# The end of a mixture-of-experts stage: stored expert rows fetched and summed during the last expert, its own rows placed by one-hot products

## The reference

```python
def moe_swiglu(h, w_router, wg, wu, wd):
    logits = (h @ w_router).astype(jnp.float32)
    top_v, top_i = lax.top_k(logits, TOP_K)              # TOP_K = 2 of 8 experts
    w_top = jax.nn.softmax(top_v, axis=-1)
    gate = jnp.sum(jax.nn.one_hot(top_i, N_EXPERTS, dtype=jnp.float32) * w_top[..., None], axis=-2)
    out = jnp.zeros_like(h)
    for e in range(N_EXPERTS):
        out = out + gate[..., e:e + 1].astype(h.dtype) * swiglu(h, wg[e], wu[e], wd[e])
    return out

# in second_block, l = 1:
        h = layer_norm(ALPHA * h + f, ln2_g[l], ln2_b[l])   # f = moe_swiglu(h, ...)
```

## Time and profile before

| | us |
|---|---|
| median of 3 runs (lowest, highest) | 2637.42 (2636.57, 2639.19) |
| the profiled execution's own time | 2639.29 |
| its span, first to last instruction | 2637.4 |
| PE busy | 2490.1 (94%) |
| DVE busy | 1393.3 (53%) |
| ACT busy | 1031.7 (39%) |
| POOL busy | 189.7 (7%) |

### The profile page before, as it was taken

The page is one execution under the profiler, slowest core; times in us unless marked ns, Lnnn a source line. Parts: engine busy times, 40 slices in busy tenths (PEclk is TensorE's granted clock), DMA queues, the critical chain, the costliest instruction groups (busy, mean ns, idle before and its releaser), DMA issues.

```text
span 2637.4 us, 37964 instructions
## 1 busy us (share of the span) xinstructions
PE 2490.1 (94%) x15190; PEld 2017.2 (76%) x15190; DVE 1393.3 (53%) x2043; ACT 1031.7 (39%) x1402; POOL 189.7 (7%) x136
## 2 busy tenths in 40 slices
PE   8999999998999999999899999988988999999993
PEld 6888888776788887877668888777765888888882
DVE  5433445565443345466453323356655666666666
ACT  4222234334322223345442212233553555566552
POOL 1000010000000002200130000220002000000000
PEclk9999999999999999999999999999998999999997
DMA  4222222101222221321112322222113577777773
GB/s 151 103 104 80 108 102 100 67 28 47 95 103 104 80 108 68 108 95 49 48 64 96 112 80 103 88 88 100 49 39 154 214 268 268 275 281 273 272 270 139
DMA packets 50752, 328.36 MB, mean 124 GB/s; under 512 B 5857, under 2 KB 5985, under 8 KB 19169
## 3 DMA queue, kind: packets, MB, share of 16 engines
q1 hardware_dynamic: 45184, 310.60, 32.0%
q0 software_dynamic: 4032, 13.88, 1.5%
q10 hardware_dynamic: 1440, 2.57, 0.3%
HBM read 317.58 MB, written 9.44 MB: 124 GB/s over the span
## 4 chain that ended last, share of the span: by engine, by line
PE 83%; DVE 8%; ACT 3%; DMA 3%; issue 2%; POOL 0%; DVEq 0%; ACTq 0%; POOLq 0%; SPq 0%
PE ps L2301 16%; PE ps L2303 16%; PE ps L2302 16%; PE ps L912 5%; PE ps L1521 2%; PE ps L1505 2%; PE ps L1522 2%; PE ps L1523 2%; DMA expert_rows<-y_tail,sidx 2%; PE ps L1560 2%; PE ps L417 1%; PE ps L1547 1%; PE ps L1561 1%; PE ps L1562 1%; PE ps L967 1%
## 5 line engine op out<-in xcount | busy, mean ns | idle before, releaser
L2301 PE MATMUL ps<-xh,wh 128*128 128x512 f32 x1344 | 532.7, 396 | 39.3 <-DVE xl L2157 14.0
L2302 PE MATMUL ps<-xl,wh 128*128 128x512 f32 x1344 | 528.5, 393 | 0.0
L2303 PE MATMUL ps<-xh,wl 128*128 128x512 f32 x1344 | 528.2, 393 | 0.0
L1892 DVE TENSOR_TENSOR wl<-raw,wh 128x2048 fp32r<-128x2048 f32 (+3 forms) x137 | 331.0, 2416 | 144.8 <-ACT wh L1887 144.8
L1887 ACT CAST wh<-raw 128x2048 fp32r<-128x2048 f32 (+3 forms) x137 | 270.2, 1972 | 325.6 <-PE ps L2303 291.3
L1748 DVE TENSOR_TENSOR wml<-raw_m,wmh 128x2048 fp32r<-128x2048 f32 (+1 forms) x146 | 307.1, 2113 | 162.7 <-ACT wmh L1607 161.3
L2301 PEld LDWEIGHTS ps<-xh,wh 128*128 128x128 f32 x1344 | 255.8, 190 | 100.1 <-issue 23.4
L1607 ACT CAST wmh<-raw_m 128x2048 fp32r<-128x2048 f32 (+1 forms) x146 | 258.7, 1773 | 187.0 <-PE ps L1505 113.7
L2302 PEld LDWEIGHTS ps<-xl,wh 128*128 128x128 f32 x1344 | 256.1, 191 | 54.2 <-issue 1.0
L2303 PEld LDWEIGHTS ps<-xh,wl 128*128 128x128 f32 x1344 | 255.7, 190 | 54.3
L2301 PE MATMUL ps<-ah,wh 128*128 128x512 f32 x528 | 206.2, 391 | 0.0
(11 more groups left out here) (379 smaller groups left out, 3945.6 us busy)
## 6 DMA issues: line engine op xcount, KB each, us to landing
raw_m<-in_moe SPq DMA_DIRECT2D x104, 1024.0 KB, 5.2
raw<-in_ffn_up SPq DMA_DIRECT2D x65, 1024.0 KB, 4.8
raw_m<-in_moe SPq DMA_DIRECT2D x32, 768.0 KB, 4.6
raw<-in_in SPq DMA_DIRECT2D x20, 1024.0 KB, 4.8
raw<-in_ffn_down SPq DMA_DIRECT2D x12, 1536.0 KB, 6.5
raw<-in_ffn_down SPq DMA_DIRECT2D x12, 1280.0 KB, 5.3
raw<-in_cmp SPq DMA_DIRECT2D x8, 1024.0 KB, 4.7
raw<-in_out SPq DMA_DIRECT2D x8, 1024.0 KB, 4.8
```

Of the source, the lines that this page charges most:

```text
L1892: nc.vector.tensor_tensor(wl[:, slot, 0:size], raw[:, slot, 0:size], wh[:, slot, 0:size].bitcast(F32), ALU.subtract).then_inc(lo_ready, 1)
L2301: nc.tensor.matmul(dst, hi_w, hi_x, start=(k == 0), stop=False)
L2302: nc.tensor.matmul(dst, hi_w, lo_x, start=False, stop=False)
L2303: return nc.tensor.matmul(dst, lo_w, hi_x, start=False, stop=(k == last_k))
```

## The change

- **Clearing.** POOL fills one half of a new tile `yin` with zeros behind its first gather. SP, behind the load of item 6 of pass 0, writes the zeros over all 1024 rows of `expert_rows` in eight transfers, 4.19 MB. POOL waits for them before the first scatter.
- **ALPHA.** POOL multiplies the four tiles of `xtok` by ALPHA, also behind its first gather.
- **Placing.** In every pass DVE makes, in `current()`, from the scatter's row numbers the token number of each row (`at_row`, three dependent steps) and two matrices of 128 by 512 that hold a 1 where a column's number is the row's token (`onehot`, one for full rows, one for tail rows). Only those of the last pass are used.
- **The last pass is taken out of the loops** of ACT, DVE and POOL. ACT and DVE leave out the two splits that nothing uses. POOL does not scatter.
- **Fetching.** SP reads the stored rows when the scatter of the last pass but one has landed and the last item's load has been issued, into the two halves of `yin`. POOL adds them to `xtok`, eight additions of 128 by 1024, during the last pass. The third tile's read waits for the first tile's sums, the fourth's for the second's.
- **Summing in PSUM.** Behind its loop PE brings `xtok` into PSUM by products with the identity (`residual`), and adds the last pass's rows by products of `onehot` with `y_rows` and `y_tail`. DVE takes the statistics and the first step of the layer norm straight from PSUM. Its two additions per tile go.

```diff
@@ SP @@
                 load(0, n)
+                if n == RAWS:
+                    sp.wait_ge(y_added, 1)
+                    for part in range(2 * NT):
+                        sp.dma_start(y_dram[part * P:(part + 1) * P], yin[:, 0, 0]).then_inc(y_cleared, 16)
...
-            for n in range(2):
-                sp.wait_ge(e_done, last * NI + (NI + n - RAWS + 1))
-                sp.sem_inc(e_raw[n], 16)
-            sp.wait_ge(e_scatter, passes * 32)
+            sp.wait_ge(e_scatter, last * 32)
+            sp.wait_ge(y_cleared, 16 * 2 * NT)
             for tt in range(NT):
+                if tt >= 2:
+                    sp.wait_ge(y_added, 2 * tt)
                 for c in range(2):
-                    sp.dma_start(raw_m[:, 2 + tt, c * D:(c + 1) * D],
-                                 y_dram[c * S + tt * P:c * S + (tt + 1) * P]).then_inc(y_loaded[tt], 16)
+                    sp.dma_start(yin[:, tt % 2, c], y_dram[c * S + tt * P:c * S + (tt + 1) * P]).then_inc(y_loaded[tt], 16)
@@ POOL @@
+            gather()
+            nc.gpsimd.memset(yin[:, 0, 0], 0.0).then_inc(y_added, 1)
+            for tt in range(NT):
+                ins = nc.gpsimd.tensor_scalar(xtok[:, tt], xtok[:, tt], ALPHA, None, ALU.mult)
+            ins.then_inc(y_added, 1)
...
+            with pool.Fori(0, passes - 1) as p:
+                gather_next(p)
+                pool.wait_ge(y_cleared, 16 * 2 * NT)
...
+            gather_next(pool.value_load(plan[0:1, 1, NP_AT:NP_AT + 1], min_val=NE - 1, max_val=NE + EXTRA - 1))
+            pool.wait_ge(y_added, 2)
+            for tt in range(NT):
+                pool.wait_ge(y_loaded[tt], 16 + 32)
+                for c in range(2):
+                    nc.gpsimd.tensor_tensor(xtok[:, tt], xtok[:, tt], yin[:, tt % 2, c], ALU.add).then_inc(y_added, 1)
+                    pool.wait_ge(y_added, 3 + 2 * tt + c)
@@ PE, behind its loop @@
+            def residual(tt):
+                pe.wait_ge(y_added, 4 + 2 * tt)
+                for half in range(2):
+                    nc.tensor.matmul(ps[:, AT_BANK[tt] + half], ident, xtok[:, tt, half * S:(half + 1) * S], start=True, stop=False)
+            residual(0)
+            residual(1)
+            pe.wait_ge(e_y_dve, passes)
+            pe.wait_ge(e_y_act, passes + 1)
+            for tt in range(NT):
+                tok = slice(tt * P, (tt + 1) * P)
+                if tt >= 2:
+                    residual(tt)
+                for half in range(2):
+                    nc.tensor.matmul(ps[:, AT_BANK[tt] + half], onehot[:, 0, tok], y_rows[:, half * S:(half + 1) * S], start=False, stop=False)
+                for g in (0, 2, 1, 3):
+                    if g == 1:
+                        pe.wait_ge(f_part, 2 * tt + 2)
+                    rows = slice(32 * g, 32 * g + 32)
+                    mm = nc.tensor.matmul(ps[:, AT_BANK[tt] + g // 2, (g % 2) * 256:(g % 2) * 256 + 256], onehot[rows, 1, tok], y_tail[rows],
+                                          start=False, stop=(g % 2 == 1))
+                    if g % 2 == 0:
+                        mm.then_inc(f_part, 1)
+                mm.then_inc(f_sum, 1)
@@ ACT and DVE @@
-                    else:
+                    elif not final:
                         split(p, n + 2 - NI, 1)
@@ DVE, in current() @@
                     nc.vector.tensor_tensor(sidx[:], nxt[:, 2], tab["shift"], ALU.add).then_inc(e_sidx, 1)
+                    chain_row(nc.vector.tensor_tensor(at_row[:, 0], nxt[:, 1], tab["empty"], ALU.subtract), 0)
+                    chain_row(nc.vector.tensor_scalar(at_row[:, 1], at_row[:, 0], float(S), -float(S), ALU.is_ge, ALU.mult), 1)
+                    chain_row(nc.vector.tensor_tensor(at_row[:, 2], at_row[:, 0], at_row[:, 1], ALU.add), 2)
+                    for part in range(2):
+                        nc.vector.tensor_scalar(onehot[:, part], tab["tokens"], at_row[:, 2, part:part + 1], None, ALU.is_equal)
@@ DVE, behind its loop @@
-                dve.wait_ge(y_loaded[tt], 32)
-                chain.then(nc.vector.scalar_tensor_tensor(xtok[:, tt], xtok[:, tt], ALPHA, raw_m[:, 2 + tt, 0:D], ALU.mult, ALU.add))
-                chain.then(nc.vector.tensor_tensor(xtok[:, tt], xtok[:, tt], raw_m[:, 2 + tt, D:2 * D], ALU.add))
+                dve.wait_ge(f_sum, tt + 1)
                 for half in range(2):
-                    ins = nc.vector.bn_stats(bn[:, tt, half], xtok[:, tt, half * S:(half + 1) * S])
+                    ins = nc.vector.bn_stats(bn[:, tt, half], ps[:, AT_BANK[tt] + half])
```

More of the change, by code:

```diff
@@ L248, in build @@
             bn = sb("bn", [P, NT, 2, 6], on=moe)
+            yin = sb("yin", [P, 2, 2, D], on=moe)
+            onehot = sb("onehot", [P, 2, S], on=moe)
+            at_row = sb("at_row", [P, 3, 2], on=moe)
             mv = sb("mv", [P, NT, 4], on=moe)
@@ L1407, in gather, with gather_next @@
                                         bass.IndirectOffsetOnAxis(ap=gidx[0:TAIL, 1:2], axis=0)).then_inc(e_gather, 16)
[L1409 to L1414, removed]
+            def gather_next(p):
                 pool.wait_ge(e_gidx, p + 2)
@@ L1418, in pool_moe @@
                 gather()
+            pool.wait_ge(e_gidx, 1)
+            pool.wait_ge(rows_stored, 16 * NT)
+            gather()
[3 more added lines that the diff above has]
+            ins.then_inc(y_added, 1)
+            pool.wait_ge(m_list, 1)
+            passes = pool.value_load(plan[0:1, 0, NP_AT:NP_AT + 1], min_val=NE, max_val=NE + EXTRA)
+            with pool.Fori(0, passes - 1) as p:
+                gather_next(p)
+                pool.wait_ge(y_cleared, 16 * 2 * NT)
                 pool.wait_ge(e_y_act, p + 2)
@@ L1592, in pe_moe @@
                 down_full(UPS + 5).then_inc(e_done, 1)
+            passes = pe.value_load(plan[0:1, 0, NP_AT:NP_AT + 1], min_val=NE, max_val=NE + EXTRA)
+            pe.wait_ge(e_xlo, passes * 2 + 2)
+            def residual(tt):
[21 more added lines that the diff above has]
+                mm.then_inc(f_sum, 1)
         def act_moe(act, chain):
@@ L1622, in act_moe, with one_pass @@
             passes = act.value_load(plan[0:1, 0, NP_AT:NP_AT + 1], min_val=NE, max_val=NE + EXTRA)
-            with act.Fori(0, passes) as p:
+            def one_pass(p, final):
                 def silu(grp):
@@ L1653, in act_moe @@
                 nc.scalar.activation(y_tail[:], ps[:, 3, 0:256], ACT.Copy, scale=cur[:, 1:2]).then_inc(e_y_act, 1)
+            with act.Fori(0, passes - 1) as p:
+                one_pass(p, False)
+            one_pass(act.value_load(plan[0:1, 1, NP_AT:NP_AT + 1], min_val=NE - 1, max_val=NE + EXTRA - 1), True)
             act.preload_act_table_set(LN_EXP)
@@ L1764, in dve_moe, with one_pass @@
             passes = dve.value_load(plan[0:1, 0, NP_AT:NP_AT + 1], min_val=NE, max_val=NE + EXTRA)
-            with dve.Fori(0, passes) as p:
+            def one_pass(p, final):
                 def glu(grp):
@@ L1817, in dve_moe @@
                 nc.vector.tensor_scalar(y_rows[:, S:D], ps[:, 7], cur[:, 0:1], None, ALU.mult).then_inc(e_y_dve, 1)
+            with dve.Fori(0, passes - 1) as p:
+                one_pass(p, False)
+            one_pass(dve.value_load(plan[0:1, 1, NP_AT:NP_AT + 1], min_val=NE - 1, max_val=NE + EXTRA - 1), True)
             def finish(tt):
                 dve.wait_ge(f_rstd, tt + 1)
-                chain.then(nc.vector.scalar_tensor_tensor(xtok[:, tt], xtok[:, tt], mv[:, tt, 0:1], lastrow[:, 0:D],
+                chain.then(nc.vector.scalar_tensor_tensor(xtok[:, tt], flat(ps[:, AT_BANK[tt]:AT_BANK[tt] + 2]), mv[:, tt, 0:1], lastrow[:, 0:D],
                                                           ALU.subtract, ALU.mult))
```

17 lines of the change are left out of this document (12 added, 5 removed).

## The result

| | before | after |
|---|---|---|
| median of 5 runs (lowest, highest), us | 2637.32 (2636.57, 2639.19) | 2652.76 (2647.91, 2657.45) |
| the profiled execution's own time | 2639.29 | 2652.76 |
| its span | 2637.4 | 2650.9 |
| mean granted clock | 0.977 | 0.980 |

The ratio is 1.0057, with a 95% interval of 1.0046 to 1.0069. The forecast was 2640.1 and its range ended at 2650: the time lies outside. Between the two profiled executions the spans differ by 13.5 us, and that is what the profile has to explain. The mean clock is of no help: it is a mean over the whole program, and PE now works where it stood idle before, in the last of the 40 slices of the profile's page (its row PEclk ends with 9, that of before with 7).

The account below looks back on a forecast made before the run. PE bounds the passes, tied to the scatter before item 4; latencies and DVE bound the end. 2.3 + 0.7 + 2.0 + 7 x 1.41 + 0.3 - 12.5 = +2.7 us: 2640.1 from the median, range 2630 to 2650.

Parts of the forecast that it names:

- where the slack is nought: DVE between `cur` and item 4's split: anything added there lengthens seven of eight passes by its whole length.
- the size of the work: One-hot work on DVE in each pass: three small steps and two comparisons, 1.41 us, bounds 1.3 and 1.8.
- the whole of it counts, seven times: 9.9: PE's wait before item 4: the 1.41 us of one-hot work lengthens seven passes, 9.9 us in all.
- rival 1: PE's clock falls behind the longer wait before item 4 in each of seven passes: +11 us, 2651; chance 0.14.
- the end: Behind PE's last expert product: sums on PE, which sets the pace; gain 12.5 us, bounds 14 and 9.
- rival 4: POOL's additions take 3.7 and push the fourth tile's sum past PE's need: +5 us, 2645; chance 0.10.
- POOL against DVE in pass 0: POOL's first multiplication gets between DVE's splits of items 0 and 1; PE starts 2.3 us later, bounds 0 and 3.5.
- In the last pass: A POOL addition can stand in front of DVE's splits of items 15 and 16: 0.3 us, bounds 0 and 2.
- The zeros: 4.19 MB in SP's queue ahead of item 7's load in pass 0 delay PE: loss 2.0 us, bounds 0 and 13.
- Rival 3: Transfers and locks are dearer: zeros at 250 GB/s (+5.6), POOL entering at each split: 2647; chance 0.16.
- Rival 2: Something else ends PE's wait before item 4, so 9.9 becomes 3 or less: 2633 or 2630; chance 0.14.

Follow-up runs that it names:

- the first four experiments: After, one-hot in last pass only: 2639.01; before plus one-hot work: 2661.09; before plus two comparisons only: 2651.49; after plus two unused PE products inside the wait: 2643.26 us.

## Why the prediction was wrong

**Right: where the slack is nought, and the size of the work.** The chain was read rightly: all that was put between `cur` and the split of item 4 counts in each pass. 1.35 us against 1.41.

**Wrong: what the work costs PE.** The step that failed is "the whole of it counts, seven times: 9.9". It took the price of a longer wait to be its length. With the wait at 1.96 or more the clock fell to its lower level behind six of seven, for 1.5 us each: 9.2 us for which the sum had nothing. That was rival 1, with its price (1.6) right, and given 0.14. That its 2651 lies so near to 2652.8 is in part luck: it had seven falls for six, and no late landings. The argument against it was that in the earlier trace rows narrow products stood ahead of the idle time and in the passes 24 full ones, and that waits up to 1.2 had left the clock alone. The first doesn't matter, as the kernel before with the one-hot work shows (24 full products ahead, clock fallen seven times of seven). The second said nothing of 2.2: the only idle time of that length in my rows was followed by 0.50. I had a row for the length I predicted and set it aside for rows of half the length.

**Missing: the late landings.** With the slack at nought the pass is exposed to every scatter that lands late. Two at 8.7 cost 3.2 us. The kernel before is exposed too, and its one profile showed seven landings within 0.6; I took their spread for that. It would have belonged in the range, on the upper side alone. This is the second term that the sum put at nothing.

**Right: the end.** 11.9 gained for 12.5. The pairs of tail products do lie over one another: eight instructions of 256 columns in 1.50 (1.36 predicted with the waits between, 2.22 one by one). A tile takes PE 5.06 for 4.8, and DVE waits 1.05 for it, so PE sets the pace, as worked out. POOL's additions end 9.4 us behind PE's last expert product (about 10 predicted), and PE never waits for them; an addition is 2.4 for 2.6. With that rival 4 falls.

**Right in kind, too large: POOL against DVE in pass 0.** The Trainium skill's page SBUF — State Buffer, section SBUF: two separate sides, has the exclusive lock go to whichever instruction starts first. The trace agrees in part: the cast, recorded behind the start of POOL's clearing, took 1.60 for 0.17, and POOL's second multiplication, recorded while the first split ran, took 5.38 for 2.8. But POOL's first multiplication (2.84) and DVE's first split (2.27) lie beside each other for 1.8 us in the record, and neither is longer than alone by more than 0.04. My error was in the order, and in the size of a multiplication (2.8 for 3.1). I had POOL enter between two splits that stand back to back on DVE; it didn't. 0.4 for 2.3.

**In the last pass** PE waited 0.69 and 0.34 for splits beside the additions, 1.0 for the predicted 0.3, inside the bounds of 0 and 2.

**The zeros** were 1.5 for 2.0. That they cost 3.4 when `current()` is behind the split of item 6 shows that the term is a meeting of two times, and that a wait of 2.18 pays for the clock here too. Rival 3 (zeros at 250 GB/s, POOL entering at each split) falls: DMA stood at 379 to 412 GB/s from 2060 to 2085, and POOL did not enter between the splits of pass 0.

**Rival 2** (something else ends the wait) falls: DVE's split ended it seven times of seven.

Sum of the errors: +12.1 in the passes, +0.9 in the last pass, -2.8 in pass 0 and +0.6 at the end give the 10.8 between 13.5 and 2.7. The medians stand 15.4 apart, since the profiled execution of before was 2.0 over its own median of five and that of after is its median.

## What to carry to other kernels

Price a longer wait of PE at its length plus what the clock takes behind it, and look for an idle time of the predicted length in the trace, not for the nearest one in the same loop: here 1.35 us of work on DVE cost 2.9 in each pass in which the clock fell. Work that one engine must do once a pass belongs where that engine idles; moving `current()` three items on made the one-hot work, the clock and the late landings free all at once. It was worth 9 us in the kernel before, and the change beside it some 5 to 7. A transfer that many passes wait for without slack is a risk even when its profile looks steady.

## What the runs showed of the chip that I had not expected

- In six kernels (before, after and the first four experiments), one profiled execution of each, there are 42 waits in front of item 4 of passes 1 to 7. None of the 23 waits up to 1.74 us was followed by a lower clock, and 16 of the 19 from 1.93 us on were, with a mean of 0.69 to 0.72 over the next 5.5 us. The exceptions were 2.12, 2.55 and 3.00. What they had in common stays open. The kernel without the unused splits adds seven waits, up to 1.61, and no fall. PE's waits for a load in pass 0 fit: 1.16 without a fall, 2.04 and 2.18 with one.
- The scatter of 128 and 32 rows landed after 7.0 to 8.2 us in most passes of these six (in two after 6.0 and 6.3, issued later) and after 8.6 to 8.9 in seven of 42. A late landing does not need the one-hot work: one was late (8.63) in a pass without it. Its cause stays open.
- A cast of 32 numbers on DVE took 1.60 us beside POOL's clearing of 128 x 1024 and the start of its first multiplication, and 0.17 without them. So an instruction can lose nine times its length, however small it is.
